# Turned value products, two-pass gate sums and 512-column gate and up products in a two-block transformer kernel

## The reference, cut to what matters

```python
# head C (X and Y: without cum, over the memory); G has no gate
s = einsum('bhqd,bhkd->bhqk', qb, k) * scale + (cqb[..., :, None] - cum[:, :, None, :])
p = softmax(where(causal, s, -inf))
o = einsum('bhqk,bhkd->bhqd', p, v)
y = concatenate([yc * silu(cz), yx * silu(xz)], axis=-1)
return h + y @ w_out
...
def swiglu_ffn(x, w_gate, w_up, w_down):      # width 1024 -> 2816 -> 1024, twice
    return (silu(x @ w_gate) * (x @ w_up)) @ w_down
```

## Time and profile before

| | us |
|---|---|
| runs | 1394.54, 1398.10, 1399.53 |
| median | 1398.10 |
| profiled execution | 1399.62 |
| its span | 1397.8 |
| PE, DVE, ACT busy in it | 1326.4, 859.2, 656.6 |

### The profile page before, as it was taken

The page is one execution under the profiler, slowest core; times in us unless marked ns, Lnnn a source line. Parts: engine busy times, 40 slices in busy tenths (PEclk is TensorE's granted clock), DMA queues, the critical chain, the costliest instruction groups (busy, mean ns, idle before and its releaser), DMA issues.

```text
span 1397.8 us, 23384 instructions
## 1 busy us (share of the span) xinstructions
PE 1326.4 (95%) x9398; PEld 1244.5 (89%) x9398; DVE 859.2 (61%) x1171; ACT 656.6 (47%) x994; POOL 61.5 (4%) x72
## 2 busy tenths in 40 slices
PE   6999997999999998989998899899999998899996
PEld 6999997889998887879998798899999897899995
DVE  6566676775765444479978655655556755555555
ACT  5445676454436666346433444344443343333431
POOL 0012011000110000000000000100000100000000
PEclk9999999999989999989999999899999999899998
DMA  7555433345544332545534543655555453455552
GB/s 238 169 190 183 153 121 121 123 157 177 180 137 134 98 114 91 202 129 165 167 98 151 179 149 124 227 191 191 182 180 181 129 173 121 145 187 181 181 186 83
DMA packets 167925, 219.71 MB, mean 157 GB/s; under 512 B 3691, under 2 KB 151478, under 8 KB 167846
## 3 DMA queue, kind: packets, MB, share of 16 engines
q1 hardware_dynamic: 164502, 206.68, 45.3%
q0 software_dynamic: 3040, 11.20, 2.6%
q10 hardware_dynamic: 304, 0.73, 0.1%
HBM read 217.54 MB, written 1.05 MB: 156 GB/s over the span
## 4 chain that ended last, share of the span: by engine, by line
PE 80%; DVE 11%; ACT 4%; DMA 3%; issue 2%; POOL 0%; DVEq 0%; SPq 0%; ACTq 0%
PE bank L498 23%; PE bank L499 23%; PE bank L500 23%; DVE w_lo L1629 3%; PE bank L747 2%; DVE small L1653 1%; ACT w_hi L1098 1%; DVE h L1770 1%; PE bank L707 1%; PE bank L726 1%; DVE att L1691 1%; PE bank L759 1%; DMA w_raw<-in_o_w_out 1%; DMA w_raw<-in_e_w_mem_kv 1%; PE bank L666 1%
## 5 line engine op out<-in xcount | busy, mean ns | idle before, releaser
L1629 DVE TENSOR_TENSOR w_lo<-w_raw,w_hi 128x1024 fp32r<-128x1024 f32 x388 | 472.0, 1223 | 383.0 <-ACT w_hi L1098 379.7
L1098 ACT ACTIVATE w_hi<-w_raw 128x1024 fp32r<-128x1024 f32 x388 | 408.6, 1057 | 472.0 <-PE bank L500 367.5
L498 PE MATMUL bank<-u_hi,w_hi 128*128 128x256 f32 x1088 | 314.7, 289 | 3.3 <-DVE u_lo L1751 3.3
L499 PE MATMUL bank<-u_lo,w_hi 128*128 128x256 f32 x1088 | 311.8, 287 | 0.0
L500 PE MATMUL bank<-u_hi,w_lo 128*128 128x256 f32 x1088 | 311.7, 286 | 0.0
L498 PE MATMUL bank<-w_hi,u_hi 128*128 128x256 f32 x832 | 239.1, 287 | 2.2 <-DVE w_lo L1629 2.2
L498 PE MATMUL bank<-w_hi,y_hi 128*128 128x512 f32 (+1 forms) x656 | 235.3, 359 | 3.7 <-DVE w_lo L1629 3.7
L500 PE MATMUL bank<-w_hi,u_lo 128*128 128x256 f32 x832 | 236.6, 284 | 0.0
L499 PE MATMUL bank<-w_lo,u_hi 128*128 128x256 f32 x832 | 236.5, 284 | 0.0
L499 PE MATMUL bank<-w_lo,y_hi 128*128 128x512 f32 (+1 forms) x656 | 231.5, 353 | 0.0
L500 PE MATMUL bank<-w_hi,y_lo 128*128 128x512 f32 (+1 forms) x656 | 231.2, 352 | 0.0
(11 more groups left out here) (275 smaller groups left out, 1306.6 us busy)
## 6 DMA issues: line engine op xcount, KB each, us to landing
w_raw<-in_e_w_in SPq DMA_DIRECT2D x28, 1024.0 KB, 5.1
w_raw<-in_o_w_in SPq DMA_DIRECT2D x28, 1024.0 KB, 5.2
w_raw<-in_ffn_wg SPq DMA_DIRECT2D x22, 1024.0 KB, 5.3
w_raw<-in_ffn_wu SPq DMA_DIRECT2D x22, 1024.0 KB, 5.4
w_raw<-in_ffn_wd SPq DMA_DIRECT2D x22, 1024.0 KB, 4.8
w_raw<-in_ab_w_in SPq DMA_DIRECT2D x12, 1024.0 KB, 5.1
w_raw<-in_e_w_out SPq DMA_DIRECT2D x8, 1024.0 KB, 5.0
w_raw<-in_o_w_out SPq DMA_DIRECT2D x8, 1024.0 KB, 5.0
```

What stands on the lines that cost most here:

```text
L498: pe.matmul(out_ap, ah, bh, start=start, stop=False, skip_group_check=True)
L499: pe.matmul(out_ap, ah, bl, start=False, stop=False, skip_group_check=True)
L1098: act.activation(w_hi[:, at:at + 1024], w_raw[:, at:at + 1024], ACT.Copy).then_inc(hi_done, 1)
L1629: v.tensor_tensor(w_lo[:, at:at + 1024], w_raw[:, at:at + 1024], w_hi[:, at:at + 1024].bitcast(F32), ALU.subtract).then_inc(lo_done, 1)
```

## The change

1. **Gate and up units of the feed-forward.** `u_hi` and `u_lo` become two halves of one tile `u_s`. A new `half_unit` streams both under one load of `w_hi` in one matmul of 512 columns (two runs of 256), then hi x lo of the weights with 256 columns: two matmuls in place of three, and the same number of columns. hi and lo sums land in separate halves of a bank, so gate takes banks 0 and 1 and up 6 and 7 in every step. ACT copies the left halves (`part`), DVE adds the right ones (`both`), ACT takes silu from SBUF.
2. **Turned value products** for X, C, Y and G: V is stationary and the turned probabilities move, so the output is already turned. `st_turn_y` remains for A alone. The scale by 1/sum moves to the probabilities, in `st_combine`, ahead of their turn, so turn_p now waits for `a_pn`. The gates `eXZ`, `oZ` and `oXZ` are computed turned (weights stationary). For G nothing is left of `st_y`.
3. **Sums of the forget gate in two passes.** `cumT` is split into `cum_hi` and `cum_lo`; q x k comes first, then four fp32r matmuls of 12 rows.
4. **Cross attention.** All stages of head h stand in the middle of a unit (`stages`): values of h-2, scores of h, turn_p of h-1. The values and the split of the outputs come one or half a unit later than before. xo's first bank is 7 in place of 2.

The diff, cut to its core:

```diff
-                    pick = ident[0:12, hd:hd + 1].to_broadcast([12, P])
-                    pe.matmul(b[:, 0:P], q[:, 0:P], k[:, 0:P], start=True, stop=False)
-                    pe.matmul(b[:, 0:P], pick, cumT[:, 0:P], start=False, stop=True)
-                    pe.matmul(b[:, P:384], q[:, P:SEQ], k[:, :], start=True, stop=False)
-                    mm = pe.matmul(b[:, P:384], pick, cumT[:, :], start=False, stop=True)
+                    row = pick[0:12, hd:hd + 1].to_broadcast([12, P])
+                    pe.matmul(b[:, 0:P], q[:, 0:P], k[:, 0:P], start=True, stop=False, skip_group_check=True)
+                    pe.matmul(b[:, P:384], q[:, P:SEQ], k[:, :], start=False, stop=False, skip_group_check=True)
+                    for part in (cum_hi, cum_lo):
+                        last = part is cum_lo
+                        pe.matmul(b[:, 0:P], row, part[0:12, 0:P], start=False, stop=last, skip_group_check=True)
+                        mm = pe.matmul(b[:, P:384], row, part[0:12, :], start=False, stop=last, skip_group_check=True)
...
             def st_turn_p(g):
-                if kind == "A":
-                    pe.wait_ge(a_pn, g + 1)
-                else:
-                    pe.wait_ge(a_ex, g + 1)
+                pe.wait_ge(a_pn, g + 1)
...
             def st_values(g):
+                if kind == "G":
+                    pe.wait_ge(a_yl, g)
+                    for j in range(2):
+                        cs = slice(SEQ * hd + P * j, SEQ * hd + P * j + P)
+                        for k in range(2):
+                            mm = pe.matmul(o[:, SEQ * j:SEQ * j + SEQ], V2[:, k, cs], p[:, SEQ * k:SEQ * k + SEQ],
+                                           start=(k == 0), stop=(k == 1))
...
+                elif kind == "C":
+                    pe.matmul(o[:, 0:SEQ], v[:, 0, cs], p[:, 0:SEQ], start=True, stop=False, skip_group_check=True)
+                    mm = pe.matmul(o[:, P:SEQ], v[:, 1, cs], p[:, SEQ:384], start=False, stop=True, skip_group_check=True)
                 else:
+                    for k in range(2):
+                        mm = pe.matmul(o[:, 0:SEQ], v[:, k, cs], p[:, SEQ * k:SEQ * k + SEQ], start=(k == 0), stop=(k == 1))
...
             def st_turn_y(g):
+                if HEADS[g][0] != "A":
+                    return
...
             def cross(layer):
+                def stages(h):
+                    if 0 <= h - 2:
+                        st_values(g + h - 2)
+                    if h < 4:
+                        st_scores(g + h)
+                    if 0 <= h - 1 < 4:
+                        st_turn_p(g + h - 1)
                 query(0, fresh=(end - 1, end))
...
+                query(1, between=lambda: stages(0))
+                query(2, between=lambda: stages(1))
+                query(3, between=lambda: stages(2))
+                output(0, between=lambda: stages(3))
+                output(1, between=lambda: stages(4))
+                output(2, between=lambda: stages(5))
                 output(3)
...
+                def half_unit(slot, banks, half):
+                    for m in range(2):
+                        for k in range(4 * half, 4 * half + 4):
+                            a = 2048 * slot + SEQ * k + P * m
+                            pe.matmul(two(bank[banks[m]][:, :], SEQ), w_hi[:, a:a + P], u_both[:, :, SEQ * k:SEQ * k + SEQ],
+                                      start=(k == 0), stop=False, skip_group_check=True)
+                            mm = pe.matmul(bank[banks[m]][:, 0:SEQ], w_lo[:, a:a + P], uh[:, k, :],
+                                           start=False, stop=(k == 7), skip_group_check=True)
+                    mm.then_inc(half_done, 1)
...
# ACT
+                def part(dst, par, banks, signal):
+                    for m in range(2):
+                        at = 512 * par + SEQ * m
+                        ins = act.activation(dst[:, at:at + SEQ], bank[banks[m]][:, 0:SEQ], ACT.Copy)
+                    ins.then_inc(signal, 1)
+                def gate(par, count):
+                    act.wait_ge(evacuated, kb - hs + count)
+                    s = SG[:, 512 * par:512 * par + 512]
+                    act.activation(s, s, ACT.Silu).then_inc(gate_on, 1)
...
# DVE
-                    v.reciprocal(rinv[g % 4][:, 0:2], rsum[p][:, 0:2]).then_inc(a_pn, 1)
+                    mark(v.reciprocal(rinv[g % 4][:, 0:2], rsum[p][:, 0:2]))
+                    wait_own()
+                    first = P if HEADS[g][0] == "C" else SEQ
+                    for m, b in enumerate((slice(0, first), slice(first, 384 if first == P else 512))):
+                        ins = v.tensor_scalar(Sb[p][:, b], Sb[p][:, b], rinv[g % 4][:, m:m + 1], None, ALU.mult)
+                    ins.then_inc(a_pn, 1)
...
+                    gate = {"X": eXZ, "C": oZ, "Y": oXZ}[kind]
+                    v.tensor_tensor(ys[p][:, 0:SEQ], bank[OB][:, 0:SEQ], gate[:, hd, :], ALU.mult).then_inc(a_yn, 1)
...
+                def both(dst, par, banks):
+                    for m in range(2):
+                        d = dst[:, 512 * par + SEQ * m:512 * par + SEQ * m + SEQ]
+                        ins = v.tensor_tensor(d, d, bank[banks[m]][:, SEQ:2 * SEQ], ALU.add)
+                    return ins
+                def gate_in(par, count):
+                    v.wait_ge(gate_part, count)
+                    both(SG, par, (0, 1)).then_inc(evacuated, 1)
+                def hidden(par, count):
+                    v.wait_ge(up_part, count)
+                    both(HF, par, (6, 7)).then_inc(up_sum, 1)
+                    v.wait_ge(up_sum, count)
+                    v.wait_ge(gate_on, count)
                     f = HF[:, 512 * par:512 * par + 512]
+                    v.tensor_tensor(f, SG[:, 512 * par:512 * par + 512], f, ALU.mult).then_inc(ff_a, 1)
```

More of the change, by code:

```diff
@@ L775, in attention @@
                         kb = BANK0[phase] + j
-                        k8_unit(u % 2, kb % 2, uh, ul, name == "e" and j >= 4, 2 * u + 1, kb - 1)
+                        gate = name == "o" and (j - before >= C_HEADS or (j - before) % 2)
+                        k8_unit(u % 2, kb % 2, uh, ul, gate or (name == "e" and j >= 4), 2 * u + 1, kb - 1)
                     elif kind == "DN":
@@ L826, in gate_up @@
+                def gate_up(off, lo_w, ev_w, up_w, fresh=None):
+                    for half in range(2):
+                        if fresh is not None:
+                            pe.wait_ge(tL, fresh[half])
+                        pe.wait_ge(lo_done, lo_w + half)
+                        if half == 0:
+                            pe.wait_ge(evacuated, ev_w)
+                        half_unit((base + off) % 2, (0, 1), half)
                     for half in range(2):
                         pe.wait_ge(lo_done, lo_w + 2 + half)
-                        for m in range(2):
-                            for k in range(4 * half, 4 * half + 4):
-                                a = 2048 * slot + SEQ * k + P * m
-                                mm = passes(bank[bk][:, SEQ * m:SEQ * m + SEQ],
-                                            ((w_hi[:, a:a + P], w_lo[:, a:a + P]), (uh[:, k, :], ul[:, k, :])),
-                                            half == 0 and m == 0 and k == 0, k == 7)
@@ L834, in gate_up @@
-                        mm.then_inc(half_done, 1)
+                        if half == 0 and up_w is not None:
+                            pe.wait_ge(up_sum, up_w)
+                        half_unit((base + off + 1) % 2, (6, 7), half)
                 hs = layer * FFN_STEPS
                 end = turned(f"xa{layer}")
-                gate_up(0, 0, 2 * base + 1, kb - 1, (end - 1, end))
+                gate_up(0, 2 * base + 1, kb, hs if hs else None, (end - 1, end))
                 def pair(i, first):
@@ L1335, in ffn @@
                 base, kb = UNIT0[name], BANK0[name]
-                def gate(par):
-                    def go(b):
-                        act.activation(SG[:, 512 * par:512 * par + 512], bank[b][:, :], ACT.Silu).then_inc(evacuated, 1)
-                    return go
+                hs = layer * FFN_STEPS
+                def part(dst, par, banks, signal):
[7 more added lines that the diff above has]
+                    act.activation(s, s, ACT.Silu).then_inc(gate_on, 1)
                 def pair(i):
@@ L1407, in _ @@
             stream("e_nat", 10, 4, nat_dst(eZ), ACT.Silu)
-            stream("e_nat", 14, 2, nat_dst(eXZ), ACT.Silu)
+            stream("e_nat", 14, 2, t_dst(eXZ), ACT.Silu)
             stream("e_bz", 0, 2, t_dst(eBZ), ACT.Silu)
@@ L1946, in two_ahead @@
                     lo_of(u + 2, 0)
-                    if h is not None:
+                    if h is not None and h < 4:
                         st_combine(g + h)
+                    if h is not None and h >= 2:
+                        st_y_lo(g + h - 2)
                     lo_of(u + 2, 1)
@@ L1973, in ffn @@
                 hs = layer * FFN_STEPS
-                def hidden(par, gate, up):
```

(17 more changed lines are left out.)

175 lines of the change are left out of this document (78 added, 97 removed).

## The result

| | this kernel, us (runs) | the kernel before, same chip | ratio, 95% |
|---|---|---|---|
| the change | 1380.74 (1378.12 to 1384.16, 4) | 1398.82 | 0.9876 [0.9858, 0.9894] |
| the change, measured again | 1382.57 (1382.30 to 1383.85, 5) | 1396.33 | 0.9900 [0.9883, 0.9918] |

A forecast was written before the change was run, and what follows sets the result against it. PE was taken as the bound, with room on DVE and ACT. Terms of -8.4, +1.0, -3.7, -2.7, -5.0, -2.0 and -0.5 sum to -21.3 us from the profiled 1399.6, forecast 1378 us, range 1369 to 1389.

The forecast's parts named there:

- C scores: Scores of the 12 C heads: 1.98 us a head falls to 1.5 to 1.6, -5.0 us in all.
- gate and up pairs: Feed-forward gate and up units: 704 groups of matmuls go from 0.360 to 0.348 us each, -8.4 us.
- ends of the layers: Last feed-forward step of each layer: new copies and additions delay the last down unit, +0.5 a layer, +1.0 us.
- turned outputs beside units: Attention outside the cross attentions: 34 transposes of 0.108 us go, -3.7 us; the added DVE scales are covered.
- cross attentions: Both cross attentions: 32 transposes -3.5, fewer float32/fp32r changes -0.8, four waits for y_lo +1.6, together -2.7 us.
- odd bare steps: Odd layer's steps without units: output units start earlier, partly lost if the clock falls, -2.0 us (-3 to 0).
- even bare steps: Even layer's steps without units: shorter wait for y -0.85, scale of head 8 delays by 0.35, -0.5 us.
- rival A: Gate and up units: the surcharge belongs to each run of 256 columns, costing 8.4 us: 1387 us, chance 0.15.
- the 0.8 for fewer changes of format: Cross attentions: the gap after a plain float32/fp32r change (about 0.08) is met once, not twice, in some units, -0.8 us.
- the bound with 128 columns at a quarter of the pace: C-head scores: if 128 columns of fp32r run at a quarter of the pace, 1.83 us a head, gain only 1.8.
- Rival B: 12-row loads hide and the bare-step clock holds: 3 more at scores, 1 in steps, 1 in cross stages; 1373, chance 0.12.
- Rival C: Longer chains bite: +2 in each cross attention, +1 at each layer end, +2 in bare steps; 1386 us, chance 0.12.

## Why the prediction was right, and where it was off

The mechanism was right: PE is the bound, DVE and ACT have room, and nearly every us off PE is off the end. The time lies in the range, the forecast 2.7 below the median of the first measurement and 4.6 below that of the second. That it is so near is in part luck: the largest term was mis-sized by half, and the C scores brought 2.0 more than their term. Term by term:

| term | forecast | the traces show |
|---|---|---|
| gate and up pairs | -8.4 | -4.1 |
| ends of the layers | +1.0 | +0.7 |
| turned outputs beside units | -3.7 | -3.4 |
| cross attentions | -2.7 | -1.3 |
| C scores | -5.0 | -7.0 |
| odd bare steps | -2.0 | -2.5 |
| even bare steps | -0.5 | +0.7 on average, not told apart |
| wait ahead of the first feed-forward | none | +0.9 |
| sum | -21.3 | -16.0 |

The two measurements give -18.1 and -13.8, with -16.0 between.

- **Gate and up units.** This term was mis-sized by half. The step that failed is "because the 512-column row is the same number of columns into a bank": its 0.228 is the pitch of a wide matmul among wide ones. 19 of the 24 had that pitch, the first five 0.232. The step lands in the middle between forecast and rival A, for a reason that neither names.
- The Trainium skill's gap (page "TensorE: Matmul & The Clock Gate", section "Back-to-back issue gap"), which that page gives for an isolated matmul and by which the gain was to be 1.8 us, is too low by 2.3, the forecast too high by 4.2: 4.1 to 4.2 measured. The surcharge over the columns is 0.013 here where it has 0.0025.
- **Turned outputs.** The price of a transpose, 0.108, holds (18 x 0.108 = 1.9, and 0.15 for the values). The count was nearly right: 30 of the 34 stand where PE doesn't wait, 18 beside units and 12 among the output units (1.3 in sum), and 4 in bare steps. What the prediction has no term for is the longer wait ahead of the first feed-forward layer, 0.9.
- **Cross attention.** The transposes bring 1.65 in each, 1.75 by the forecast, and the new waits cost 0.81, to the tenth the 2 x 0.4 of the forecast. What failed is the 0.8 for fewer changes of format. The changes do save about 0.4 in each, but three of the four blocks of scores now stand ahead of a turn and take 1.73 where they took 1.54, 0.57 in each, which takes back more than that: -1.65 + 0.81 + 0.57 - 0.4 comes to the -0.65 of each.
- **C scores.** Once the products of 12 rows stand together, the second part of 128 columns takes 0.06 of the 0.16 that I gave it, little over the 0.053 of its columns, so its load hides. With that the bound with 128 columns at a quarter of the pace fell too. Rival B's two conditions both came true, this one and the clock in the bare steps, with 2.0 and 0.5 more than the forecast and not 3 and 1; its gain in the cross attentions did not come.
- **Bare steps.** The longest wait of PE fell from 4.26 to 2.95, "about 3". From 540.2 to 555.0 it was 14.8 us before, with the clock at 0.77; now 12.5 at 1.00. In ten traces with turned outputs and new C scores, the stretch from the last matmul ahead of these steps to L502 is 14.49 or 14.50 us; 15.21 with C scores undone, 16.48 with turned outputs undone, 17.01 before. In the even layer PE's first wait grew instead, from 2.98 to 3.65. Before (DVE, POOL) and after:

```profile
231.72 1.20 DVE L1629 TENSOR_TENSOR w_lo<-w_raw,w_hi 128x1024 fp32r<-128x1024 f32 x1
```

```profile
232.38 0.59 POOL L1564 TENSOR_SCALAR small<-small 128x2 f32<-128x2 f32 x1 [5.88 <-ACTq L1269]
```

```profile
232.36 0.62 DVE L1885 TENSOR_SCALAR att<-att,small 128x256 f32<-128x256 f32 x2
232.89 1.22 DVE L1675 TENSOR_TENSOR w_lo<-w_raw,w_hi 128x1024 fp32r<-128x1024 f32 x1
```

```profile
232.91 1.26 POOL L1610 TENSOR_SCALAR small<-small 128x2 f32<-128x2 f32 x1 [5.89 <-ACTq L1290]
```

The two scales put w_lo 0.6 later behind y_hi's chain, and POOL's step for the last A head's product, two columns wide, ends 0.05 after w_lo in both. I had 0.35 for this. At the end PE's wait of 0.70 is down to 0.17. Over the whole stretch the traces scatter by 2.4 us, and what the edit does to its sum stays open.
- **Rival C** was right on the waits in the cross attentions, and at the layers' ends in kind; inside the layers it fell.

## What to carry to other kernels

Read the pitch of an instruction in the company that it will have, not as the mean of a row: the first few behind a different size told here what half a term was worth. When wide and narrow matmuls must both run, put the wide ones together. And count what an edit removes stretch by stretch, since what goes from a place where the engine waits brings nothing.

## What the runs showed of the hardware

- Pitches at full clock (granted 1.00, 2.4 GHz) for fp32r, 128 rows, a new weight load for each: 0.120 for 256 columns among their like, 0.2267 for 512 among theirs, 0.020 more for each change from narrow to wide, whether the moving operand is one run of 512 columns or two of 256.
- At the lower clock there is no surcharge. Changed kernel, start of the second feed-forward layer, with a granted clock of 0.50 (1.2 GHz):

```profile
1183.29 0.63 PE L836 MATMUL bank<-u_s,w_hi 128*128 128x512 f32 x1
1183.72 0.41 PE L838 MATMUL bank<-u_s,w_lo 128*128 128x256 f32 x1
1183.93 0.63 PE L836 MATMUL bank<-u_s,w_hi 128*128 128x512 f32 x1
```

A pair takes 0.640, which is 768 columns at 1.2 GHz; three narrow ones take the same there, so the wide matmul brings nothing while the clock is low.
- A POOL operation of 2 columns took 0.59 us where it began 0.55 before DVE's w_lo ended and 1.26 where both began together; it ended with w_lo both times. The Trainium skill, page "SBUF — State Buffer", section "🔬 SBUF: two separate sides", says that a DVE operation with two inputs in SBUF and a POOL operation that reads SBUF lock each other out, the second waiting to the end of the first. Both rows agree with it; no run was made on that alone.
- Ahead of the odd bare steps, the same distance of 3.22 us between PE's starts left the clock at 1.00 in the changed kernel, and lowered it with the C scores undone (0.74 over the stretch). What decided isn't shown.
